# Page products in four strips of the TensorE array, and six value page pairs beside the heads

## The reference

```python
PAST_LEN = 1024; PAGE_SIZE = 128          # 8 pages a sequence, 8 sequences
k_past = cache_moba_k[:, page_table].reshape(N_ODD, Bs, past, H_C, HD_C)
v_past = cache_moba_v[:, page_table].reshape(N_ODD, Bs, past, H_C, HD_C)

def moba_attend(q, k_all, v_all, pos0, rel_bias):
    kb, vb = blocks(k_all), blocks(v_all)              # blocks of 256 keys, two pages
    kmean = jnp.mean(kb.astype(jnp.float32), axis=3)
    gate = jnp.einsum('blhd,bhnd->bhln', q, kmean)     # past blocks only
    top_s, top_i = lax.top_k(gate, MOBA_TOPK)          # three blocks and the own one
    ...
    s = jnp.einsum('hqd,hqnkd->hqnk', qq, ksel) * scale + bias
    p = jax.nn.softmax(s.reshape(H, qb, -1), axis=-1).reshape(s.shape)
    return jnp.einsum('hqnk,hqnkd->hqd', p, vsel)
```

## Time and profile before

| | |
|---|---|
| median of three runs | 1109.22 us |
| profiled execution, its own time | 1111.75 us |
| its span, first to last instruction | 1109.9 us |
| mean granted TensorE clock | 0.965 |
| PE (TensorE) busy | 1053.0 us, 95% |
| DVE (VectorE) busy | 658.8 us, 59% |
| ACT (ScalarE) busy | 387.0 us, 35% |
| page loads | 64 of keys and 64 of values, 256.0 KB each, 3.7 and 3.4 us to landing |

### The profile page before, as it was taken

How to read it: one execution, slowest core, us unless ns; L and a number is a source line. 1 busy time by engine, 2 the same in 40 slices (tenths; PEclk the granted TensorE clock), 3 DMA queues, 4 the chain that set the end, 5 groups by cost and what they waited for, 6 DMA issues and landing times.

```text
span 1109.9 us, 20548 instructions
## 1 busy us (share of the span) xinstructions
PE 1053.0 (95%) x8212; PEld 896.2 (81%) x8212; DVE 658.8 (59%) x1417; ACT 387.0 (35%) x722; POOL 102.1 (9%) x202
## 2 busy tenths in 40 slices
PE   7998999999998999999999898799999899999996
PEld 5877988877885999999987553367788689999996
DVE  5865716245333798986656565367241468998652
ACT  3533222522144544435322112332223454444330
POOL 0010002320000022120000000000100001212100
PEclk9997999969999999999999999889999999999999
DMA  8321124413744555564355877764844635555540
GB/s 332 130 104 40 42 81 152 152 45 114 303 163 178 180 173 186 190 219 187 135 176 189 326 235 224 239 188 177 313 148 146 233 112 170 182 190 198 189 152 40
DMA packets 41568, 192.42 MB, mean 173 GB/s; under 512 B 4602, under 2 KB 5754, under 8 KB 24578
## 3 DMA queue, kind: packets, MB, share of 16 engines
q1 hardware_dynamic: 36146, 167.39, 43.5%
q0 software_dynamic: 4288, 22.15, 5.2%
q10 hardware_dynamic: 1040, 1.57, 0.4%
HBM read 183.74 MB, written 7.35 MB: 172 GB/s over the span
## 4 chain that ended last, share of the span: by engine, by line
PE 73%; issue 10%; SPq 5%; DVE 5%; DMA 3%; ACT 2%; POOL 0%; DVEq 0%; ACTq 0%; POOLq 0%
PE bank L1270 72%; SPq L658 3%; SPq L644 3%; DVE work L1953 2%; ACT work L814 1%; DMA ring<-in_ck 1%; DMA ring<-in_od_in 1%; DVE work L1956 1%; PE bank L1273 1%; DMA x<-in_x 1%; ACT work_r L814 1%; DMA ring<-in_pool_v 0%; DVE work L2727 0%; DVE ring_r L1953 0%; DVE sq L1953 0%
## 5 line engine op out<-in xcount | busy, mean ns | idle before, releaser
L1270 PE MATMUL bank<-h,ring 128*128 128x264 f32 x896 | 209.3, 390 | 0.6 <-DMA ring<-in_od_in 0.6
L1270 PE MATMUL bank<-h_r,work_r 128*128 128x264 f32 x704 | 200.5, 285 | 0.0
L1270 PE MATMUL bank<-h_r,ring_r 128*128 128x264 f32 x704 | 200.2, 284 | 0.0
L1270 PE MATMUL bank<-sq_r,work_r 128*128 128x264 f32 x704 | 199.8, 284 | 0.0
L1270 PEld LDWEIGHTS bank<-h,ring 128*128 128x128 f32 x896 | 170.2, 191 | 34.3 <-issue 5.5
L814 ACT ACTIVATE work_r<-ring 128x2048 fp32r<-128x2048 f32 (+1 forms) x60 | 125.0, 2087 | 191.0 <-PE bank L1270 191.0
L1953 DVE TENSOR_TENSOR ring_r<-ring,work_r 128x2048 fp32r<-128x2048 f32 (+1 forms) x60 | 150.2, 2506 | 45.3 <-ACT work_r L814 45.2
L1270 PE MATMUL bank<-work_r 128*128 128x264 f32 x704 | 129.7, 285 | 3.3 <-DVE ring_r L1953 3.1
L1270 PEld LDWEIGHTS bank<-sq_r,work_r 128*128 128x128 f32 x704 | 132.5, 188 | 0.1
L1270 PEld LDWEIGHTS bank<-h_r,ring_r 128*128 128x128 f32 x704 | 132.4, 188 | 0.0
L1270 PEld LDWEIGHTS bank<-h_r,work_r 128*128 128x128 f32 x704 | 132.3, 188 | 0.1
(11 more groups left out here) (255 smaller groups left out, 1125.0 us busy)
## 6 DMA issues: line engine op xcount, KB each, us to landing
ring<-in_gu SPq DMA_DIRECT2D x44, 1024.0 KB, 4.8
ring<-in_down SPq DMA_DIRECT2D x16, 1408.0 KB, 6.0
ring<-in_pool_k SPq DMA_DIRECT2D x64, 256.0 KB, 3.7
ring<-in_pool_v SPq DMA_DIRECT2D x64, 256.0 KB, 3.4
ring<-in_ev_in_a SPq DMA_DIRECT2D x8, 1024.0 KB, 7.1
ring<-in_ev_in_b SPq DMA_DIRECT2D x8, 1024.0 KB, 4.9
work<-in_cv POOLq DMA_DIRECT2D x8, 1024.0 KB, 12.9
ring<-in_ck SPq DMA_DIRECT2D x8, 1024.0 KB, 4.9
```

The lines of the kernel that those rows point to most:

```text
L1270: return nc.tensor.matmul(out, lhsT, rhs, start=start, stop=stop, skip_group_check=True)
```

## The change

A key slot now holds two sequences with two pages (one block) each, so a pair holds four sequences and its products use all four strips: 16 products of 256 columns for keys, eight of 512 for values. A value bank then collects four sequences over two pairs, which is half of their pages; the two halves lie in two banks. ScalarE copies the first (now 128 partitions, after head steps 4 and 8), VectorE adds the second (`second_half`). Value pairs 4 and 5 move from scan steps 0 and 2 to head steps 7 and 8, pairs 6 and 7 from scan steps 4 and 6 to scan steps 0 and 1. The number of page slots, transfers and register loads is the same.

```diff
@@ make_plan: pages, and the scan steps
-        elif i < 7:
+        elif i < 9:
             value_pages(i - 3)
...
-        if i % 2 == 0:
-            value_pages(4 + i // 2)
+        if i < 2:
+            value_pages(i + 6)
@@ SyncE, a page slot
-                    if name == "pk":
-                        i = 2 * (4 * (i // 8) + i % 4) + i // 4 % 2
-                    else:
-                        i = 2 * (2 * (i // 4) + i % 2) + i // 2 % 2
+                    s0_, b_ = 4 * (i // 8) + 2 * (i % 2), i // 2 % 4
                     numbers = [sp.value_load(pages[0:1, at:at + 1], min_val=0, max_val=POOL_PAGES - 1)
-                               for at in range(4 * i, 4 * i + 4)]
+                               for s_ in (s0_, s0_ + 1) for at in (PAGES * s_ + 2 * b_, PAGES * s_ + 2 * b_ + 1)]
@@ ScalarE, samples_out
-                r = 64 * (i % 2)
-                drain(f(dst[r:r + 64, i // 2, :], bank(key)[r:r + 64, :], ACT.Copy), key)
+                drain(f(dst[:, i // 2, :], bank(key)[:, :], ACT.Copy), key)
...
-                if i in (4, 6):
+                if i in (4, 8):
                     samples_out(osm, i // 2 - 2)
...
-                if i in (3, 7):
-                    samples_out(osm, 2 + i // 4)
@@ TensorE, key_pages
-                r = [slot("pk", n)[:, 0:2048].rearrange("p (g c t) -> p g c t", g=4, c=HC) for n in pair]
+                r = [slot("pk", n)[:, 0:2048].rearrange("p (s g c t) -> p s g c t", s=2, g=2, c=HC) for n in pair]
+                part = slice(256 * (i % 2), 256 * (i % 2) + 256)
                 for c in range(HC):
-                    for n in pair:
-                        s_, j = 4 * (n // 8) + n % 4, n % 4
-                        ins = mm(b[32 * j:32 * j + 32, :], qz[:, c, s_, :], r[n % 2][:, :, c, :],
-                                 c == 0, c == HC - 1)
-                        if c == HC - 1:
-                            slot_done(ins, "pk", n)
+                    for j in range(4):
+                        ins = mm(b[32 * j:32 * j + 32, part], qz[:, c, 4 * (i // 4) + j, :],
+                                 r[j // 2][:, j % 2, :, c, :], c == 0, c == HC - 1)
+                        if c == HC - 1 and j % 2:
+                            slot_done(ins, "pk", pair[j // 2])
@@ TensorE, value_pages (both call sites move as in make_plan)
-                if i % 4 == 0:
-                    for j in (i // 2, i // 2 + 1):
-                        drained(pe, ("pt", "moba", j))
+                if i % 2 == 0:
+                    drained(pe, ("pt", "moba", i // 2))
                 n = 2 * i
                 key = ("so", "moba", n // 4)
                 b = open_(key) if n % 4 == 0 else bank(key)
-                half = n // 2 % 2
-                r = [slot("pv", n + m) for m in range(2)]
-                for g in range(4):
-                    for m in range(2):
-                        s_ = 2 * (n // 4) + m
-                        j = s_ % 4
-                        ins = mm(b[32 * j:32 * j + 32, :], spt[2 * (s_ // 4) + half][:, g, j, :],
-                                 r[m][:, 512 * g:512 * g + 512], half == 0 and g == 0, half == 1 and g == 3)
-                        if g == 3:
-                            slot_done(ins, "pv", n + m)
+                r = [slot("pv", n + m)[:, 0:2048].rearrange("p (s g e) -> p s g e", s=2, g=2) for m in range(2)]
+                for g in range(2):
+                    for j in range(4):
+                        ins = mm(b[32 * j:32 * j + 32, :], spt[i // 2][:, 2 * (i % 2) + g, j, :],
+                                 r[j // 2][:, j % 2, g, :], i % 2 == 0 and g == 0, i % 2 == 1 and g == 1)
+                        if g == 1 and j % 2:
+                            slot_done(ins, "pv", n + j // 2)
@@ VectorE
+            def second_half(g):
+
+                key = ("so", "moba", 2 * g + 1)
+                full(dve, key)
+                drained(dve, ("so", "moba", 2 * g))
+                drain(tt(osm[:, g, :], osm[:, g, :], bank(key)[:, :], ALU.add), key)
+
...
                 if i == 7:
+                    second_half(0)
                     weigh_blocks()
...
+                if i == 3:
+                    second_half(1)
                 if i >= 3 and i % 2:
                     y_out((i - 3) // 2)
```

## The result

The change makes the kernel slower: 1121.24 us (median of 4 runs, 1119.99 to 1124.19) against 1108.85 us (4 runs, 1107.28 to 1109.3), a ratio of 1.0118, 95% interval 1.0087 to 1.0149. The profiled execution took 1122.43 us (span 1120.6), 10.7 us more than that of before. TensorE is busy 1041.2 us of it (93%), 11.8 us less than before, at a mean clock of 0.948 instead of 0.965.

The account below looks back on a forecast made before the run. It took SP's slot issuing to bound the heads and VectorE the scan. A scan end 10.0 us later, added to the profiled 1111.75, gave 1121.8; less 2.5 for the runs' median, 1119.2 us, range 1116.5 to 1122.

Parts of the forecast that it names:

- The scan is bounded by VectorE, with TensorE only just on the path: Scan before the change: VectorE's steps follow at 4.40 us, with waits for scan inputs of only 0.84 and 1.00 us.
- A product in four strips takes 1.93 us: Key and value page products on TensorE: 1.93 us instead of 3.63, 1.70 us less for each of 16 pairs.
- SP's unbroken run starts 1.7 us earlier: Key pairs 0 to 4: one faster product brings SP's run forward 1.7 us, to 634.95; bounds nothing to 9.0.
- SP's pace hides the products in the heads: Key pairs 5 to 7, value pairs 0 to 3: no gain, SP needs 4.29 to 4.56 us a slot.
- Pair 5 delays the scan's start, harmlessly: Head step 8: pair 5 lands at 726.3 ahead of the last PT; scan starts at 733.5 against 729.23, without harm.
- Pair 7 lands at 744.0 and holds y_pair(0) and x_pair(3): Scan steps 0 and 1: TensorE stops for pair 7's pages, giving VectorE a new 7.0 us stall before step 3.
- the 12 that the prediction named as its sign: TensorE's waits on value pages were to exceed 12 us in all, the longest ahead of pair 7.
- From step 3 on 25.6 us: Rest of the scan: 25.0 us without the two old waits, plus 0.61 for the added bank; end at 778.2.
- The rival of the clock: Idle time before pairs 5 to 7 leaves later scan products at half clock: 1122.6 to 1126.4 us, chance 0.20.
- The first rival: Value pages come in time, pair 7 landed by 733.0: 2.9 us faster than before, 1106.3 us, chance 0.07.
- The rival of strips that don't run side by side: Products reading two slots stay at 3.63 us, and SP's run starts where it did: 1122.6 us, chance 0.05.
- The rival of a larger gain in the early stage: 4 to 9 us won before 636.65, pair 7 landing 2.3 to 7.3 us earlier: 1112 to 1117 us, chance 0.18.

Follow-up runs that it names:

- before_two_queues: The kernel before (two strips, old places), with GpSimd issuing every second page slot of the head steps: 1108.93 us, ratio 0.9995 to before.
- late_tail: The changed kernel with value pairs 6 and 7 in scan steps 1 and 3 and the second added bank in step 4: 1115.44 us, ratio 1.0049 to before.
- two_queues: The changed kernel with GpSimd reading page numbers and issuing every second page slot from key slot 9 on: 1108.2 us, ratio 1.0006 to before.
- fixed_pages: The changed kernel with pages 0 to 63 in order, without register loads or run-time addresses: 1101.8 us, ratio 0.9942 to before.
- run 4: Not a follow-up run: the words are "SP's run 4 us before 636.65", meaning SP's unbroken run of page slots and a time of 4 us.
- place_only: The kernel before with its two-strip products, value pairs at the change's new places, no added banks: 1123.42 us, ratio 1.0124 to before.

## Why the prediction was right or wrong

The forecast was slower, 1119.2 us, 10.0 us above before. Measured were 1121.24 us, within its range, and 12.4 us above before. Profile against profile it was 1121.8 forecast and 1122.43 measured. Its steps:

- *The scan is bounded by VectorE, with TensorE only just on the path.* Too strong. Before, the chain lies on TensorE for 20.92 us of the scan's 39:

```profile
735.18 20.92 PE bank L1270 x272
```

VectorE's waits are as short as the prediction says, so the two bounds are close there.

- *A product in four strips takes 1.93 us.* Right: 1.92 to 1.93 behind other work. It also runs side by side from two slots, so that rival falls.
- *SP's unbroken run starts 1.7 us earlier.* Not borne out by this pair of profiles. It starts at 636.34 against 636.65. The gain was there at the weight slot ahead of it, which starts at 615.31 instead of 617.29, and was gone at its landing, 628.67 instead of 628.98, with the transfer engines full from 615 to 629 us. They were as full before: the stretch of rows 5 lies behind that landing, but the row of the landing itself says the same, a share of 1.03:

```profile
617.00:629.00 12.00, 8.26 (x37) 4.64 (x35) 5.14 (x13) 1.09 (x4) 1.08 (x2) 1.00 1.03 378
```

The lower bound of the prediction, that they eat the 1.7, is what this pair of profiles shows. Over all profiles with register loads this start lies at 636.65, 638.27 and 637.89 with two strips, and at 636.34, 635.36, 639.10, 637.27, 638.00, 638.66 and 630.88 with four. It scatters by 8 us where the code up to there is nearly the same, so 1.7 can't be read from one pair of profiles.

- *SP's pace hides the products in the heads.* Right: 4.35 us a slot, between the 4.29 and 4.56 of the prediction, and strips_only, the change without the new places, is 0.2% below before, with an interval that just holds no change. What the prediction didn't see is how close the other bound was: it called SP the bound, and TensorE with two strips was nearly as strong a one (before_two_queues).
- *Pair 5 delays the scan's start, harmlessly.* The start came at 730.77, not 733.5. Pair 5 ran at 725.06 without a wait, where its pages had been forecast for 726.3 (with the median landing of 3.2 us, though a slot needs its last transfer, up to 4.3 us in rows 4); pair 4's new wait on VectorE's addition took 3.06 us, the upper end given (3 us at half clock). Harmless is right for the change as it stands, since the pages of pair 7 set the end; late_tail, where that stall is gone, still loses 0.0049.
- *Pair 7 lands at 744.0 and holds y_pair(0) and x_pair(3).* Right in its mechanism: TensorE could use it at 742.54, and did for 3.64 us at half clock (forecast 3.86). From its start to step 3 on VectorE it took 9.04 us, forecast 8.63. Step 3 came at 751.58 (forecast 752.6) behind a wait of 7.19 us (forecast 7.0). TensorE's five waits on value pages add up to 14.1 us, above the 12 that the prediction named as its sign; but the longest is ahead of pair 3 (4.78 us), not of pair 7 (4.18). That pair 7 came so near its forecast is in part luck: SP's run began 1.4 us later than forecast (636.34 against 634.95), which slots 4.35 us apart made good, where the forecast had carried over the 4.56 of before up to pair 5.
- *From step 3 on 25.6 us.* 27.3 measured. This is the term that was too small, by 1.7 us, which is one wait of VectorE, 1.75 us at 763.35. y_pair(2) waits 3.24 us for the second added bank and then, with x_pair(5), runs in part at half clock: 756.72 to 761.91, 5.2 us, where the prediction had 3.43. The prediction had seen this wait and given it 0.4 us at full clock and 3.8 at half; it left it out, and the truth lay between. Pair 7 came 1.5 us early, what it holds took 0.4 us longer and the rest 1.7: the end of the scan, 778.87 against 778.2, is as near as it is because these partly cancel.

The rival of the clock was right in what it saw and too dear. Pairs 4, 6 and 7, each behind a wait, run at half clock, and the granted clock from 729 to 785 us is 0.85 (before, on the same window, 0.97). Yet what follows pair 7 recovers quickly: y_pair(0)'s first products take 1.85 us, where 1.41 is full speed. The Trainium skill, TensorE: Matmul & The Clock Gate, section "HAM oscillation — how this bites in real kernels", has short bursts behind waits start at half clock each time. The waits above agree, but the 1126.4 us that the prediction drew from it were not reached.

The first rival, that the pages come in time, needed pair 7 at 733.0. It came 9.5 us later. Faster issuing, which brings that rival's condition nearer, gave back 12 us in two_queues and 20 in fixed_pages, though pair 7 waits for its pages in both (3.27 and 3.86 us). The rival of strips that don't run side by side names 1.7 us and twice 1.7, which is 1124.3, not 1122.6; it fell, and nothing hangs on it. The rival of a larger gain in the early stage needed SP's run 4 us before 636.65 or more; in the profile of after it starts 0.3 before.

What stays open: how the loss splits between the end of the heads and the scan, for the steps of 0.0035 are at the edge of their uncertainty; how much of the change's own loss is the clock, which no run here took away by itself (place_only loses as much at the mean clock of before); and why the start of SP's run scatters so.

## What to carry to other kernels

Before you move work that reads loaded data to an earlier place in the queue of an in-order engine, work out from the issuing engine's pace when the data lands; everything queued behind that work waits with it, and here one stop of 4 us cost more than the 1.7 us that a faster product saves. When a part of a kernel has two bounds of about the same size, removing one can show nothing: strips or a second queue alone gave 0 to 0.2%, both together 1.0%. So test a pair of cheap changes together before you drop either, and read from the chain of waits which bound holds after each.

## What the runs showed of the hardware

With fixed page numbers it needs 1.8 us for a slot where it doesn't wait, and holds 3.3% of the chain of the heads. GpSimd issues four transfers in 2.3 us.
- With four strips the granted clock was lower where pages pace TensorE. From 650 to 725 us it is 0.87 before with TensorE busy 64.21 us, and 0.78 in strips_only, busy 56.70:

```profile
650.00:725.00 75.00, 64.21 (x397) 30.26 (x392) 34.15 (x110) 22.49 (x65) 0.00 (x0) 0.87 0.73 231
650.00:725.00 75.00, 56.70 (x442) 30.89 (x442) 31.81 (x107) 22.52 (x69) 0.00 (x0) 0.78 0.76 238
```

Over whole executions it is 0.959 to 0.973 in the 25 runs of before and 0.951 to 0.959 in the ten of strips_only. Part of the 1.7 us per product is given back so: value pairs 2 and 3 in strips_only took 3.46 and 2.58 us, not 1.92.
